# Seven half products for the first feed-forward weight too, six rotating weight buffers, and four of its weight sums made by accumulating transfers

## The reference, cut to what matters

```
def squared_relu_mlp(n, w_up, w_down):
    return jnp.square(jax.nn.relu(n @ w_up)) @ w_down

h = h + squared_relu_mlp(rmsnorm_2(h, g_ffn[layer]), w_up[layer], w_down[layer])
```

## Time and profile before

| | |
|---|---|
| median of 3 runs | 1579.47 us (1578.11 to 1579.8) |
| the profiled execution: its time, its span | 1579.45 us, 1577.6 us |
| PE busy in the span | 1559.4 us (99%) |
| DVE, ACT, POOL busy | 1036.2, 726.6, 680.8 us |
| transfers | 145.07 MB, mean 92 GB/s |

### The profile page before, as it was taken

One profiled execution on the slowest core, in us unless ns is written; L12 is line 12 of the kernel. 1 busy time (PEld: TensorE's weight loads), 2 busy tenths in 40 slices (PEclk: granted clock), 3 DMA queues, 4 the chain that ended last, 5 costly groups with the idle time before them and its releaser, 6 DMA issues.

```text
span 1577.6 us, 20552 instructions
## 1 busy us (share of the span) xinstructions
PE 1559.4 (99%) x7570; PEld 1279.8 (81%) x7570; DVE 1036.2 (66%) x1343; ACT 726.6 (46%) x1085; POOL 680.8 (43%) x666
## 2 busy tenths in 40 slices
PE   9999999999999999999999999989999999999999
PEld 8888787787778898788888888778886888888887
DVE  7434554675688977558484857877777557574847
ACT  6323433325245665345353535566765453444433
POOL 0002110104345453286665748442333574857574
PEclk9999999999999999999999999999999999999999
DMA  7232222232211211422323131222121414141321
GB/s 246 80 107 80 80 80 80 96 107 80 95 66 54 85 63 54 160 81 102 112 81 134 57 135 50 81 80 81 54 81 33 155 54 160 54 159 55 137 77 54
DMA packets 25731, 145.07 MB, mean 92 GB/s; under 512 B 3936, under 2 KB 5680, under 8 KB 9264
## 3 DMA queue, kind: packets, MB, share of 16 engines
q1 hardware_dynamic: 25648, 143.95, 26.4%
HBM read 141.84 MB, written 2.10 MB: 91 GB/s over the span
## 4 chain that ended last, share of the span: by engine, by line
PE 85%; DVE 11%; ACT 3%; issue 1%; POOL 1%; DVEq 0%; ACTq 0%; POOLq 0%
PE ps_G L613 19%; PE ps_G L614 19%; PE ps_G L615 19%; PE ps_C L1247 5%; PE ps_C L1248 5%; PE ps_C L1246 5%; DVE wide L2626 1%; DVE top L2622 1%; PE ps_AV L1076 1%; PE ps_C L699 1%; PE ps_AV L1247 1%; PE ps_AV L1246 1%; PE ps_AV L1248 1%; PE ps_AV L825 1%; PE ps_C L798 1%
## 5 line engine op out<-in xcount | busy, mean ns | idle before, releaser
L613 PE MATMUL ps_G<-ch,wh 128*128 128x512 f32 x800 | 319.9, 400 | 2.5 <-DVE wl L2221 1.8
L615 PE MATMUL ps_G<-ch,wl 128*128 128x512 f32 x800 | 312.1, 390 | 0.0
L614 PE MATMUL ps_G<-cl,wh 128*128 128x512 f32 x800 | 312.0, 390 | 0.0
L613 PE MATMUL ps_G<-nh,wh 128*128 128x512 f32 x504 | 199.7, 396 | 0.4 <-DVE h L2494 0.2
L2935 DVE TENSOR_TENSOR wl<-raw,wh 128x1024 fp32r<-128x1024 f32 (+1 forms) x104 | 179.1, 1740 | 31.0 <-ACT wh L1885 25.2
L615 PE MATMUL ps_G<-nh,wl 128*128 128x512 f32 x504 | 196.3, 390 | 0.0
L614 PE MATMUL ps_G<-nl,wh 128*128 128x512 f32 x504 | 196.2, 389 | 0.0
L613 PEld LDWEIGHTS ps_G<-ch,wh 128*128 128x128 f32 x800 | 150.6, 188 | 42.1 <-issue 7.6
L614 PEld LDWEIGHTS ps_G<-cl,wh 128*128 128x128 f32 x800 | 150.6, 188 | 33.5 <-issue 3.4
L615 PEld LDWEIGHTS ps_G<-ch,wl 128*128 128x128 f32 x800 | 150.5, 188 | 31.7
L2221 DVE TENSOR_TENSOR wl<-raw,wh 128x2048 fp32r<-128x2048 f32 x46 | 108.3, 2354 | 62.3 <-ACT wh L1388 59.2
(11 more groups left out here) (429 smaller groups left out, 3184.2 us busy)
## 6 DMA issues: line engine op xcount, KB each, us to landing
raw<-wst SPq DMA_DIRECT2D x96, 1024.0 KB, 4.9
raw<-quart_d SPq DMA_DIRECT2D x16, 1024.0 KB, 4.8
tabs<-quart_d SPq DMA_DIRECT2D x8, 1024.0 KB, 7.1
mixed_buffers<-quart_d SPq DMA_DIRECT2D x8, 1024.0 KB, 4.9
raw<-wst SPq DMA_DIRECT2D x8, 256.0 KB, 6.2
out<-wide SPq DMA_DIRECT2D x8, 256.0 KB, 2.0
h<-xT SPq DMA_DIRECT2D x7, 256.0 KB, 6.3
raw<-wst SPq DMA_DIRECT2D x2, 512.0 KB, 5.3
```

The source lines that it names most:

```text
L613: mm(o, ah, bh, start=first, stop=False)
L614: mm(o, ah, bl, start=False, stop=False)
L615: return mm(o, al, bh, start=False, stop=last)
```

## The change

The up half of a part is done by the same seven-product scheme. Its operands are quarters of the first weight (A11, A12, A21, A22: 512 inputs by 512 hidden columns) and of the input by 256 tokens and 512 inputs. The input is h times the gain alone; the root of the token is left out and comes back, squared, when a down product is added (`scalar=token_r2`, or `minus_r2` for products whose sign is turned). In a part products k = 0 to 6 are the up products, k = 7 to 13 the down products. An up product is 4 chunks x 4 blocks x 3 matmuls of 128x256 (48), in banks G0/G1 (UX), C0/C1 (UY) and C2/AV (UV).

The results are gathered in quadrants of `wide`: ScalarE copies a bank out when its quadrant is whole but for another product (`keep`), VectorE adds the other bank (`join`), and ScalarE does ReLU and square (`squared`). The value sums of the second product, 3 for each of 4 chunks, wait for `hid_set` 5g+3, so for the third of the four quadrants; 4 more come later.

Six buffers of 1 MB rotate (`WEIGHTS`; `Part.buffer`), ten quarters a part are loaded (two of them twice) in place of four tiles and four quarters. Eight weight sums are needed in a part. Four are GpSimd operations (s3, s1, t3, t1), and four (s2, s4, t2, t4) are transfers that GpSimd issues and that add one buffer to another (`accum_op=ALU.add`; s2 in two halves). The input's own sums (`enter`) are made once a layer. Both layers now start their accumulators from h, so that f = 0 gets the 32 transposes of `turn_h`, too; the token sums come from 4 small matmuls (`token_stat`).

```diff
@@ the roles of a part's 14 products
+    ROLE = ("a11", "a12", "s2", "s3", "s1", "a22", "a12", "b11", "b21", "t2", "t3", "t1", "b21", "b22")
@@ SP
+            def down_loads(pt):
+                f, p, n = pt.f, pt.p, pt.g + 1
+                split_done(pt, 0)
+                sp.wait_ge(weight_sums, 8 * n - 6)
+                load_weight(pt, "t1", quart_d[f, p, B12])
+                split_done(pt, 2)
+                sp.wait_ge(s4_in, 16 * n)
+                load_weight(pt, "b22", quart_d[f, p, B22])
+                split_done(pt, 3)
+                sp.wait_ge(s2_first, 16 * n)
+                sp.wait_ge(s2_second, 16 * n)
+                load_weight(pt, "b11", quart_d[f, p, B11])
+                split_done(pt, 5)
+                load_weight(pt, "t2", quart_d[f, p, B11])
+                split_done(pt, 6)
+                load_weight(pt, "b21", quart_d[f, p, B21])
+            def next_up_loads(pt):
+                nx, n = Part(pt.f, pt.p + 1), pt.g + 1
...
+                split_done(pt, 9)
+                sp.wait_ge(t4_in, 16 * n)
+                load_weight(nx, "a22", upq_d[f, p, A22])
+                split_done(pt, 10)
+                sp.wait_ge(t2_in, 16 * n)
+                load_weight(nx, "a11", upq_d[f, p, A11])
+                split_done(pt, 12)
+                load_weight(nx, "s2", upq_d[f, p, A22])
+                split_done(pt, 13)
+                load_weight(nx, "a12", upq_d[f, p, A12])
@@ PE
+            def up_product(pt, k, banks, fresh, x, need=lambda c: None, between=lambda c: None):
...
+                for c in range(4):
...
+                    for b in range(4):
+                        o, w = ps[banks[b // 2]][:, b % 2 * TW:(b % 2 + 1) * TW], slice(b * P, (b + 1) * P)
+                        mm(o, ah[:, c, w], xh[:, c, :], start=fresh and c == 0 and b % 2 == 0, stop=False,
+                           skip_group_check=True)
+                        mm(o, ah[:, c, w], xl[:, c, :], start=False, stop=False, skip_group_check=True)
+                        ins = mm(o, al[:, c, w], xh[:, c, :], start=False, stop=c == 3, skip_group_check=True)
@@ ACT, the stretch around the down products 7 to 10
+                    hi(5, 0)
+                    keep(3, UY, 1, 1)
+                    hi(5, 1)
...
+                    squared(1, 1, 4, -1.0)
+                    act.wait_ge(hid_set, 5 * g + 2)
+                    A(ring_hi[:, 0, :, :], quadrant(1, 1), ACT.Copy).then_inc(row_hi, 1)
+                    hi(7, 0)
+                    hi(7, 1)
+                    squared(1, 0, 6, -1.0)
...
+                    hi(9, 1)
+                    for c in range(4):
+                        act.wait_ge(value_sums, 16 * g + 3 * c + 3)
+                        A(ring_hi[:, 2:4, c, :], wide[:, 2 * c, :].rearrange("p (s n) -> p s n", s=2), ACT.Copy,
+                          scale=-1.0).then_inc(second_pair_hi, 1)
+                    hi(10, 0)
@@ POOL
-                        pool.wait_ge(hid_set, 8 * pt.g + 2 * c + 2)
...
+                    pool.wait_ge(half_lo, pt.half(1, 1))
+                    pool.wait_ge(s2_first, 16 * n)
+                    pool.wait_ge(s2_second, 16 * n)
+                    g.dma_start(s4, s2, accum_op=ALU.add).then_inc(s4_in, 16)
+                    weight_in(pt, "t1", "b22")
+                    pool.wait_ge(half_lo, pt.half(4, 1))
+                    weight_sum(t3, b22, t1_)
+                    weight_in(pt, "t2")
+                    pool.wait_ge(weight_sums, 8 * n - 2)
+                    g.dma_start(t2, t3, accum_op=ALU.add).then_inc(t2_in, 16)
+                    weight_in(pt, "b11")
+                    weight_sum(t1_, t1_, b11)
+                    pool.wait_ge(hid_set, 5 * pt.g + 3)
...
+                    for c in range(4):
+                        a11, a21, _, a22 = halves(c)
+                        value_sum(3 * c, s1[:, c, :], a22, a21, ALU.subtract)
+                        value_sum(3 * c + 1, a21, a21, a11, ALU.subtract)
+                        pool.wait_ge(value_sums, sums + 3 * c + 2)
+                        value_sum(3 * c + 2, a11, a11, s1[:, c, :], ALU.add)
+                    pool.wait_ge(half_lo, pt.half(8, 1))
+                    pool.wait_ge(t2_in, 16 * n)
+                    g.dma_start(t4, t2, accum_op=ALU.add).then_inc(t4_in, 16)
...
+                    if not pt.last:
+                        nx = Part(f, p + 1)
+                        weight_in(nx, "a11", "s1")
+                        pool.wait_ge(half_lo, pt.half(11, 1))
+                        weight_sum(weights_of(nx, "s3"), weights_of(nx, "a11"), weights_of(nx, "s1"))
+                        second_sum(nx)
+                        weight_in(nx, "a22")
+                        weight_sum(weights_of(nx, "s1"), weights_of(nx, "s1"), weights_of(nx, "a22"))
```

More of the change, by code:

```diff
@@ L670, in token_scales, with token_stat @@
                 last.then_inc(done[use[("rt", 0)][0]], 1)
+            def token_stat(n):
+                pe.wait_ge(sq_added, ADD_OF[n] + KC)
+                pe.wait_ge(st_applied, STAT[("norm", n)])
+                for t in range(NT):
+                    ins = mm(ps["ST"][:, t:t + 1], acc[0][:, t * P:(t + 1) * P], ones[:, 0:1], start=True, stop=True)
+                ins.then_inc(sq_used, 1)
             def head_stat(key):
@@ L1576, in part @@
                     for k in range(4):
-                        if k == 2 or whole and k == 0:
+                        if k == 2 and f is not None and whole:
+                            passed(act, done["G1"], st.block_use(2))
+                            for a in range(2):
+                                weight_half(Part(f, 0), 0, a)
+                        elif k == 2 or whole and k == 0:
                             split(st, k // 2)
                         stands(act, st, k)
-                        feed(n, i * 4 + k, k % 2)
+                        if f is None:
+                            feed(n, i * 4 + k, k % 2)
+                        else:
+                            feed_up(f, i * 4 + k, k % 2)
                 if name == "out1":
@@ new lines, in keep, with squared @@
+                    def keep(k, banks, row, tokens):
+                        act.wait_ge(half_done, pt.half(k, 1))
+                        for n in range(2):
+                            A(quadrant(row, tokens, n), ps[banks[n]][:].rearrange("p (c n) -> p c n", c=2),
+                              ACT.Copy).then_inc(kept, 1)
+                    def squared(row, tokens, at, scale):
+                        act.wait_ge(joined, 6 * g + at)
+                        q = quadrant(row, tokens)
+                        chain.step(A(q, q, ACT.Relu, scale=scale))
+                        A(q, q, ACT.Square).then_inc(hid_set, 1)
@@ L2483, in part @@
                             dve.wait_ge(w_lo, st.tile(2))
-                        if t or whole:
+                        if t and whole and f is not None:
+                            for a in range(2):
+                                weight_half(Part(f, 0), 0, a)
+                        elif t or whole:
                             split(st, t)
@@ new lines, in join, with add_up @@
+                    def join(k, at, banks, row, tokens):
+                        dve.wait_ge(kept, 8 * g + at)
+                        dve.wait_ge(half_done, pt.half(k, 1))
+                        for n in range(2):
+                            q = quadrant(row, tokens, n)
+                            tt(q, q, ps[banks[n]][:].rearrange("p (c n) -> p c n", c=2), ALU.add).then_inc(joined, 1)
+                    def add_up(part, i, banks, t, n, scale=token_r2):
+                        count = part.added(i) - 2
+                        dve.wait_ge(half_done, part.half(DOWN + i, 1))
```

815 lines of the change are left out of this document (486 added, 329 removed).

## The result

The changed kernel takes 1635.37 us (median, 1634.5 to 1638.26, 4 runs), the kernel before 1579.63 us on the same chip: a ratio of 1.0358, 95% interval 1.034 to 1.0376. Slower was the likeliest case of the prediction, but 1597 us was forecast and the range ended at 1625.

The account below looks back on a forecast made before the run. PE's own work was taken as the bound. From the span 1577.6: -25.5 (matmuls), +39.2 (stalls, 8 x 4.9), +4 (transposes) = 1595.3, with 1.9 around the span 1597 us; range 1556 to 1625.

Parts of the forecast that it names:

- The cadence of 0.120 us: Up products on PE: a 128x256 matmul takes 0.120 us from start to start, against 0.2267 for 128x512.
- the -25.5: Up half on PE: fewer matmul microseconds, 3.2 us saved a part, 25.5 us in eight parts.
- The mechanism: Down half, products 9 and 10: POOL's value sums make the second pair late, PE stalls 4.9 us a part.
- T: Time within a part in us, counted from PE's start of product 0; without stalls product 10 starts at 56.6.
- rival C: Accumulating transfers are slow, 12 us each, the loop 7.2 us too long; 1645 us, chance 0.18 with rival D.
- rival D: Issuing the accumulating transfers blocks POOL for several us each, five a part; 1605 to 1620 us, chance 0.18 with rival C.
- Step 5: End of a part: behind V come ACT's hi and DVE's lo; product 10 starts at V + 3.3, stall 4.9 us.
- V: End of the last of the twelve value sums that POOL makes after t1, forecast at T 58.
- Step 3: POOL's sum t1: 6.1 us plus 4 taken by DVE, T 33 to 43, quadrants done until then.
- DVE alone makes half of it: Stall at product 9: DVE's contended prices alone put its chunk 0 at 53.5 in place of 51.2.
- The other loop closes in time: Weight loop from t4's issue through s3, s2, s1, s4, b22: 47.5 us; t3 ends at 31.2, ahead of T 32.
- Rival A: Down half: POOL and DVE keep out of each other's way, no stall; 1558 us, chance 0.20.

Follow-up runs that it names:

- t1_first: Changed kernel with POOL making the sum t1 ahead of the wait for t2's load and t2's transfer issue; 1620.98 us, ratio 1.0268 to before.
- t1_wait: t1_first with POOL idle behind t4's issue until DVE has written the lo of all four second pairs; 1611.21 us, ratio 1.0208.
- keep_clock: Changed kernel with 22 useless 128x256 matmuls on PE between products 8 and 9, except in each layer's last part; 1636.18 us, ratio 1.0357.
- combo: t1_wait with DVE writing the lo of two second pairs ahead of the second half of weight 9's lo; 1606.63 us, ratio 1.0178.
- short_sums: t1_first with value sums computing only 8 columns, so other values result; 1587.63 us, one run.
- combo_both: combo_load with POOL also waiting, behind s2's issues, for the first lo half of the next part's weight 1; 1597.97 us, ratio 1.0119.
- no_t2_transfer: Changed kernel with t2's transfer left out and its semaphore raised by an instruction, so other values result; 1607.91 us, one run.
- t4_gpsimd: combo plus a POOL wait for next weight 0's lo behind s2's issues, t4 made by eight POOL additions, not a transfer; 1631.86 us, ratio 1.0334.
- combo_load: combo with SP's load of the next s1 held until t2's transfer has landed; 1600.01 us, ratio 1.0123.

## Why the prediction was wrong

**Right.** The cadence of 0.120 us and with it the -25.5. The mechanism: twelve value sums in one run, a second pair that comes too late for product 9. The times up to t2's issue, within a microsecond: t2 issued at T 32.5 (forecast 32 to 33), t1 begun at 33.1 (33). The twelve sums took 14.9 us (15.1). Of the four transfers s4 and t4, the two that the prediction's loop counts at full length, landed after 7.4 and 7.0 us (8), so rival C is out as it was put. The others were slower than 8: t2 took 11.6 us (median), outside that loop, and it costs nothing in the changed kernel's inner parts, but product 9 waits behind it once t2 is issued later (t1_first). And the issue keeps POOL for 0.88 us (1), so rival D is out in the form that I gave it.

**Step 5 failed.** "Behind V stand ACT's hi of the pair (0.6) ... and DVE's lo": product 10 started 5.8 us behind V (822.30), not 3.3 (the three terms named there make 3.0, and 58 and 3.3 make 61.3 and not 61.5, slips of 0.2 to 0.3 us). The lo of the last pair took 3.52 us, since POOL's four additions behind t4's issue held DVE; 2.5 us a part. I had priced every meeting of the two engines at 0.55 us for DVE, from rows in which POOL's queue holds no transfer. A bound from above, DVE held as long as POOL's run of additions lasts, was missing; the earlier trace rows had the length of such a run, 6.07 us.

**Step 3 failed, with the wrong sign first.** t1 took 5.9 us and ended at T 38.9, where I had 10 us and 43: POOL was not slowed by DVE, it shut DVE out. But "until then the quadrants are done (join at 36.8 to 38.1 ...)" is false for the same reason: the row's lo ahead of the join was held to T 40.0, so the value sums began at 44.6 and not at 43, V was 59.5 and not 58, and product 7 waited, which the prediction did not have at all.

Together 1.5 + 2.5 us bring the forecast start of product 10, T 61.5, to 65.5; measured 65.3. Eight parts of 4 us make 1629 of the forecast 1597. Taking both holds away (t1_wait) gave back 24 us and not 32: t2 is issued later in that order, and product 9 waits 6.7, 5.6 and 6.5 us in three parts. The rest up to 1635 is spread over the parts (the hold behind s2: 2.5 us of waits for up weights, and other parts longer than this one, 89.4 us from product 7 to product 7 in the third). The clock's fall, which I had not foreseen, is shown by keep_clock to be covered by the held pair in the part looked at; whether it costs something in the others is open.

**"DVE alone makes half of it"** (2.3 us a part, product 9 at 53.5 in place of 51.2) was priced too high as far as one run tells: combo, which lets two pairs go ahead of a weight half, won 4.6 us in eight parts.

**"The other loop closes in time"** held with little to spare. t4_late, with t4's issue moved behind four additions, costs 13.5 us.

**Rival A** (no stall, 1558) asked for POOL and DVE to keep out of each other's way, and no run here met that. What short_sums leaves after its waits and its clock is 1553, so the saving on PE that its number rests on is there.

What stays open: the last 18 us of combo_both over the kernel before. Its profile has 18.8 us of waits for the second pair, and its ACT rows show both of POOL's debts: ACT waits 3.4 us for t2 (issued at 800.83, behind the sum t1), which makes the first chunk of product 9 late, and then 1.9 us for the last value sum, which makes the last chunk late. The chain ahead of them is not POOL's sums alone. Between s4's issue and t3 POOL stands idle, since b22's load leaves only when s4 has landed:

```profile
771.52 0.88 POOL L2396 DMA_DIRECT2D raw<-raw  x1
783.72 8.63 POOL L2317 TENSOR_TENSOR tmp<-raw,mixed_buffers 128x256 f32<-128x256 f32 x8 [11.31 <-DMA raw<-quart_d]
```

s4 lands 7.1 us after its issue, the load (issued at 778.64) 5.1 us later, and then come 17.2 us of t3 and t1. So both the sums and the transfers between them seem to be the limit; no version was tried that shortens either.

## What to carry to other kernels

Before moving a sum from an engine to a transfer, look at what that engine's queue does directly behind the issue: here a transfer issued from POOL, with POOL additions behind it, held one two-input operation of DVE for 3.5 to 7.4 us, unless POOL waited between them for its own results or DVE was already at work (combo_both). Putting the additions ahead of the issue, or letting POOL wait until DVE's next operands are written, gave back 24 of the 56 us lost. And price an operation that the trace does not show by how long its neighbour's whole queue could shut others out, not by the mean slowdown of engines that take turns.

Fewer multiplications by a Winograd scheme pay only if the operands can be made ahead. In the kernel before, the lo of the four second pairs began 35, 24, 13.5 and 2.6 us before the product that uses them (i = 2). Its chunk 3, the user of the last pair, starts another 4.1 us on. The last pair's lo and the start of the product:

```profile
886.42 0.69 DVE L2935 TENSOR_TENSOR nl<-wide,nh 128x512 fp32r<-128x512 f32 x1 [0.17 <-ACT nh L1903]
```

```profile
889.06 0.39 PE L1246 MATMUL ps_C<-wh,nh 128*128 128x512 f32 x1
```

So the cover was tens of microseconds for the first pairs, as the prediction says, and 6.7 us for the last. Now all four stand on the path with no work to cover them. 25.5 us saved on PE cannot pay for 10 us of stall in each of eight parts.

## What the runs showed of the hardware

The hold. The Trainium skill (SBUF — State Buffer, "Who interferes with whom") says that DVE with two SBUF inputs and GpSimd lock each other out of a shared pair of ports, for one whole instruction, whichever starts first. The taking of turns in the earlier trace rows agrees with it. The hold does not fit: behind an issue DVE waits through four to eight instructions of 0.74 us, and without the issue (no_t2_transfer, t4_gpsimd), with a pause of 0.72 us behind it (t1_wait), or with breaks between the additions (combo_both, 2.7 us at most) it does not. Operations of DVE that read PSUM are not held: 0.73 us at 847.22, inside the run of additions that begins at 846.81. The same page has DVE starving the descriptors of transfers that GpSimd issues (the box on DVE and DMA under "SBUF: two separate sides"); the runs here show something like the opposite, and they do not show through which part it comes.

The clock. Behind waits of 2.5 us in product 9 the granted clock fell to 0.50 to 0.53. It is not always so: keep_clock has two parts with nearly the same idle time (0.98 and 0.84 us busy in 3), and the clock stayed at 1.00 behind the first and fell to 0.50 behind the second. Behind waits of 1.74 and 1.53 us (t1_first) product 9 of the inner parts stayed at 1.00.

Transfers. 1 MB added from one SBUF buffer into another landed 6.9 to 7.0 us after its issue with the load beside it moved away (t2 in combo_load). In the changed kernel, where 1 MB loads left at 795.01 and 1487.21, a quarter of a microsecond ahead of t2's issues, it took 11.5 and 12.1 us.
